# The fp32 products of a gated linear attention as f32r products of high and low parts

## What is computed

```python
proj = h @ w_in                                  # q, k, v, r, g_low
log_a = log_sigmoid(g_low @ w_gate_up + b_gate) / 16
cum = cumsum(log_a, axis=chunk);  total = cum[..., -1:, :]
k_dec = k * exp(total - cum);     chunk_decay = exp(total)
state = chunk_decay * state + k_dec^T v          # over the four chunks
o = q state                                      # then norm, silu(r), w_out
```

## Time and profile before

| | |
|---|---|
| median of 3 runs | 1426.6 us (1424.5 to 1426.8) |
| profiled execution, own time | 1427.55 us |
| its span (first to last instruction) | 1425.8 us |
| busy share of the span | PE 99%, DVE 60%, ACT 50%, POOL 2% |
| mean granted clock of TensorE | 0.997 of 2.4 GHz |
| read from HBM | 275.91 MB, 195 GB/s over the span |

### The profile page before, as it was taken

How to read it: one execution, slowest core, us unless ns; L and a number is a source line. 1 busy time by engine, 2 the same in 40 slices (tenths; PEclk the granted TensorE clock), 3 DMA queues, 4 the chain that set the end, 5 groups by cost and what they waited for, 6 DMA issues and landing times. The chain is left out here.

```text
span 1425.8 us, 17673 instructions
## 1 busy us (share of the span) xinstructions
PE 1418.1 (99%) x7202; PEld 1249.9 (88%) x7202; DVE 853.5 (60%) x889; ACT 717.9 (50%) x858; POOL 24.8 (2%) x44
## 2 busy tenths in 40 slices
PE   9999999999999999999999999999999999999999
PEld 7888888888899888998899888998888888888887
DVE  5555545655566655665555655565667786565654
ACT  6543544545545434544444534455564674665642
POOL 2000000000000000000000000000000001000000
PEclk9999999999999999999999999999999999999999
DMA  9555465657666666666666666666655556545574
GB/s 353 162 168 163 154 213 180 199 183 252 200 198 199 201 205 202 200 205 201 200 201 205 199 205 206 196 203 193 205 186 186 170 183 207 177 148 173 186 232 132
DMA packets 78016, 279.16 MB, mean 196 GB/s; under 512 B 8704, under 2 KB 9728, under 8 KB 77552
## 3 DMA queue, kind: packets, MB, share of 16 engines
q1 hardware_dynamic: 76000, 273.06, 59.4%
q0 software_dynamic: 784, 3.08, 0.6%
q10 hardware_dynamic: 1152, 1.90, 0.4%
HBM read 275.91 MB, written 2.10 MB: 195 GB/s over the span
## 5 line engine op out<-in xcount | busy, mean ns | idle before, releaser
L1020 DVE TENSOR_TENSOR w_lo<-raw,w_hi 128x1024 fp32r<-128x1024 f32 x508 | 620.0, 1224 | 521.4 <-ACT w_hi L722 517.5
L722 ACT ACTIVATE w_hi<-raw 128x1024 fp32r<-128x1024 f32 x508 | 535.0, 1056 | 642.2 <-PE banks L420 454.3
L418 PE MATMUL banks<-w_hi,xa 128*128 128x512 f32 x752 | 292.6, 389 | 0.5 <-DVE w_lo L1020 0.5
L418 PE MATMUL banks<-w_hi,xb 128*128 128x512 f32 x768 | 291.7, 380 | 0.0
L419 PE MATMUL banks<-w_lo,xb 128*128 128x512 f32 x768 | 291.1, 379 | 0.0
L420 PE MATMUL banks<-w_hi,xb 128*128 128x512 f32 x768 | 291.1, 379 | 0.0
L419 PE MATMUL banks<-w_lo,xa 128*128 128x512 f32 x752 | 285.8, 380 | 0.0
L420 PE MATMUL banks<-w_hi,xa 128*128 128x512 f32 x752 | 285.8, 380 | 0.0
L442 PE MATMUL banks<-xa,w_hi 128*128 128x512 f32 x1024 | 242.3, 379 | 0.0
L442 PEld LDWEIGHTS banks<-xa,w_hi 128*128 128x128 f32 x1024 | 184.3, 190 | 20.8
L420 PEld LDWEIGHTS banks<-w_hi,xb 128*128 128x128 f32 x768 | 145.2, 189 | 20.6
(11 more groups left out here) (196 smaller groups left out, 609.3 us busy)
## 6 DMA issues: line engine op xcount, KB each, us to landing
raw<-in_weights SPq DMA_DIRECT2D x511, 512.0 KB, 4.2
h<-in_x SPq DMA_DIRECT2D x2, 1024.0 KB, 10.1
arena<-in_x_turned SPq DMA_DIRECT2D x7, 256.0 KB, 6.3
result<-stage ACTq DMA_DIRECT2D x6, 256.0 KB, 4.7
arena<-in_final_norm POOLq DMA_DIRECT2D x1, 1024.0 KB, 7.2
raw<-in_weights SPq DMA_DIRECT2D x2, 256.0 KB, 5.0
arena<-in_gla_b_gate POOLq DMA_DIRECT2D x1, 512.0 KB, 8.5
arena<-in_lru_w_a POOLq DMA_DIRECT2D x1, 512.0 KB, 9.2
```

The source lines that it names most:

```text
L418: pe.matmul(o, xh[:, kt, xs], woven(w_hi, slot, k), start=kt == 0, stop=False)
L722: act.activation(w_hi[:, n % RING, :, :], raw[:, n % RING, :, :], ACT.Copy)\
L1020: dve.tensor_tensor(w_lo[:, n % RING, :, :], raw[:, n % RING, :, :], w_hi[:, n % RING, :, :].bitcast(F32), ALU.subtract).then_inc(lo_ready, 1)
```

## The change

All products of the four groups above become f32r products of high and low parts, and the parts have to be made:

- **Gate expansion.** ACT rounds `w_up_gate` twice, to rows 0 to 63 and 64 to 111 of `up_hi`, and DVE subtracts to `up_lo`, both at (0, 5). DVE splits `g_low` in two steps at (0, 6). Each of the four products becomes two f32r products. The load of `w_up_gate` has 64 rows instead of 48.
- **Span sums.** ACT rounds `log_a` to `la_hi` at (1, 5) and (1, 7), DVE subtracts to `la_lo` (`split_log`) at (1, 6) and (2, 0). 32 f32r products with 128 columns each (of which 7 are wanted) take the place of 16 fp32 products with 7, and move on PE from after (1, 7) to after (2, 0).
- **Suffix sums.** Eight f32r products after (2, 1), in four banks of PSUM, instead of two fp32 products after (2, 0) and two after (2, 2). ACT's exponentials move to c = 2 and 3, DVE's decayed keys to c = 3 and 4.
- **Sums over values.** ACT rounds the scores (four steps in place of two), DVE subtracts (four in place of two) one step later; ACT rounds both halves of the v panel, DVE subtracts for both. Nine f32r products for each head instead of three fp32 ones.
- GpSimd clears a larger `spans` and 32 rows of `g_low`, and casts `suffix`, at the start.

Operands that move through PE are stored or read so that neighbouring columns lie apart (`turns`, `pairs`), as those of the large products are (`woven`).

```diff
         ident = sb("ident", [P, P])
-        suffix = sb("suffix", [P, P])
+        suffix = sb("suffix", [P, P], F32R)
...
-        g_low = room(6144, S)
+        up_hi = nc.alloc_sbuf_tensor_at("up_hi", [P, 1024], F32R, offset=arena_at)
+        up_lo = nc.alloc_sbuf_tensor_at("up_lo", [P, 1024], F32R, offset=arena_at + 4 * 1024)
+        g_low = nc.alloc_sbuf_tensor_at("g_low", [P, S], F32R, offset=arena_at + 4 * 6144)
+        spans = nc.alloc_sbuf_tensor_at("spans", [P, TT, P], F32R, offset=arena_at + 4 * 14000)
+        la_hi = nc.alloc_sbuf_tensor_at("la_hi", [P, TT, 1024], F32R, offset=arena_at + 4 * 8704)
+        la_lo = nc.alloc_sbuf_tensor_at("la_lo", [P, TT, 1024], F32R, offset=arena_at + 4 * 10752)
...
-        scores = room(2816, GH, 384)
+        scores_hi = nc.alloc_sbuf_tensor_at("scores_hi", [P, GH, 384], F32R, offset=arena_at + 4 * 2816)
+        scores_lo = nc.alloc_sbuf_tensor_at("scores_lo", [P, GH, 384], F32R, offset=arena_at + 4 * 13760)
...
-        vals = room(6656, TT, N)
+        vals_hi = nc.alloc_sbuf_tensor_at("vals_hi", [P, TT, N], F32R, offset=arena_at + 4 * 6656)
+        vals_lo = nc.alloc_sbuf_tensor_at("vals_lo", [P, TT, N], F32R, offset=arena_at + 4 * 5376)
...
+        def turns(m):
+            return m.rearrange("p (a b) -> p b a", a=2)
+
+        def pairs(m):
+            return m.rearrange("p (b a) -> p b a", a=2)
+
+        SCORED = ((slice(0, 64), slice(0, S), slice(0, S)), (slice(0, 64), slice(S, S + P), slice(S + P, 2 * S)),
+                  (slice(64, 128), slice(64, S), slice(64, S)),
+                  (slice(64, 128), slice(S + 64, S + P), slice(2 * S - 64, 2 * S)))
...
             link(pool.memset(gate_w[:, :, :].bitcast(F32), 0.0))
-            pool.memset(spans[:, :, :], 0.0).then_inc(consts, 1)
-            triangle(suffix[:, :], 1.0 / 16, ALU.is_gt)
-            link(pool.affine_select(out=suffix[:, 0:CHUNK], in_=suffix[:, 0:CHUNK],
+            link(pool.memset(g_low[32:64, :].bitcast(F32), 0.0))
+            pool.memset(spans[:, :, :].bitcast(F32), 0.0).then_inc(consts, 1)
+            triangle(draft[:, 2, :], 1.0 / 16, ALU.is_gt)
+            link(pool.affine_select(out=draft[:, 2, 0:CHUNK], in_=draft[:, 2, 0:CHUNK],
                                     compare_op=ALU.is_ge, fill=0.0, base=CHUNK - 1,
...
+            pool.tensor_copy(suffix[:, :], draft[:, 2, :])
...
-            pool.dma_start(w_up_gate[0:LOW, :], w_gate_up).then_inc(up_in, 16)
+            pool.dma_start(w_up_gate[0:64, :], w_gate_up).then_inc(up_in, 16)
...
                 tt, half = divmod(i, 2)
                 if i == 0:
                     pe.wait_ge(low_out, 1)
-                    pe.wait_ge(up_in, 16)
-                pe.matmul(banks[:, gate_bank(i), :], g_low[0:LOW, tt * P:(tt + 1) * P],
-                          w_up_gate[0:LOW, half * N:(half + 1) * N], start=True, stop=True)\
-                    .then_inc(gate_ready, 1)
+                    pe.wait_ge(up_split, 1)
+                own, cols = slice(tt * P, (tt + 1) * P), slice(half * N, (half + 1) * N)
+                pe.matmul(banks[:, gate_bank(i), :], g_low[0:64 + LOW, own], turns(up_hi[0:64 + LOW, cols]),
+                          start=True, stop=False)
+                pe.matmul(banks[:, gate_bank(i), :], g_low[0:LOW, own], turns(up_lo[0:LOW, cols]),
+                          start=False, stop=True).then_inc(gate_ready, 1)

             def span_sums():
-                pe.wait_ge(log_ready, 2)
+                pe.wait_ge(gate_out, 4)
+                pe.wait_ge(la_split, 2)
                 for k in range(8):
-                    for tt in range(TT):
-                        last = pe.matmul(aux[:, 0, k * 7:(k + 1) * 7], log_a[:, tt, k * P:(k + 1) * P],
-                                         spans[:, tt, :], start=tt == 0, stop=tt == 1)
+                    for i, (part, tt) in enumerate(((la_hi, 0), (la_lo, 0), (la_hi, 1), (la_lo, 1))):
+                        last = pe.matmul(aux[:, k // 4, k % 4 * P:(k % 4 + 1) * P], part[:, tt, k * P:(k + 1) * P],
+                                         spans[:, tt, :], start=i == 0, stop=i == 3)
                 last.then_inc(span_ready, 1)

             def suffix_sums(i):
                 tt, half = divmod(i, 2)
-                if i == 0:
-                    pe.wait_ge(gate_out, 4)
-                if i == 1:
+                if i == 2:
                     pe.wait_ge(decay_ready, 1)
-                if i >= 2:
-                    pe.wait_ge(suf_out, i - 1)
-                pe.matmul(aux[:, (i + 1) % 2, :], suffix[:, :], log_a[:, tt, half * N:(half + 1) * N],
-                          start=True, stop=True).then_inc(suf_ready, 1)
+                for part in (la_hi, la_lo):
+                    last = pe.matmul(banks[:, 4 + i, :], suffix[:, :], turns(part[:, tt, half * N:(half + 1) * N]),
+                                     start=part is la_hi, stop=part is la_lo)
+                last.then_inc(suf_ready, 1)
...
-                pe.matmul(aux[:, 0, :], scores[:, hd, 0:P], vals[:, 0, :], start=True, stop=True)
-                pe.matmul(aux[:, 1, :], scores[:, hd, P:2 * P], vals[:, 0, :], start=True, stop=False)
-                pe.matmul(aux[:, 1, :], scores[:, hd, 2 * P:3 * P], vals[:, 1, :], start=False, stop=True)\
-                    .then_inc(o_ready, 1)
+                for i, tt, st in ((0, 0, 0), (1, 1, 0), (2, 1, 1)):
+                    own = slice(i * P, (i + 1) * P)
+                    for p, (s, v) in enumerate(((scores_hi, vals_hi), (scores_hi, vals_lo), (scores_lo, vals_hi))):
+                        last = pe.matmul(aux[:, tt, :], s[:, hd, own], turns(v[:, st, :]), start=p == 0 and st == 0,
+                                         stop=p == 2 and st == tt)
+                last.then_inc(o_ready, 1)
...
                     if c == 7:
                         for i in range(4):
                             gate_up(i)
-                if t == 1:
-                    if c == 7:
-                        span_sums()
                 if t == 2:
                     if c == 0:
-                        suffix_sums(0)
-                        suffix_sums(1)
-                    if c == 2:
-                        suffix_sums(2)
-                        suffix_sums(3)
+                        span_sums()
+                    if c == 1:
+                        for i in range(4):
+                            suffix_sums(i)
                     if c in (5, 7):
...
-                        act.activation(vals[:, 0, :], acc(q, 0), ACT.Copy, scale=rs[:, ST_X, 0:1])\
-                            .then_inc(acc_read_act, 1)
+                        for tt in range(TT):
+                            ins = act.activation(turns(vals_hi[:, tt, :]), pairs(acc(q, tt)), ACT.Copy,
+                                                 scale=rs[:, ST_X, tt:tt + 1])
+                        ins.then_inc(acc_read_act, 1)
                         act.wait_ge(acc_read_act, count("kqvruxKQVgl", q))
...
+                if t == 0 and c == 5:
+                    act.wait_ge(up_in, 16)
+                    act.wait_ge(tp_lo, CH)
+                    act.activation(up_hi[64:64 + LOW, :], w_up_gate[0:LOW, :], ACT.Copy)
+                    act.activation(up_hi[0:64, :], w_up_gate[0:64, :], ACT.Copy).then_inc(up_rounded, 1)
                 if t == 1:
+                    if c in (5, 7):
+                        act.wait_ge(log_ready, (c - 3) // 2)
+                        act.activation(la_hi[:, (c - 5) // 2, :], log_a[:, (c - 5) // 2, :], ACT.Copy)\
+                            .then_inc(la_rounded, 1)
...
-                    if c == 7:
+                if t == 2:
+                    if c == 1:
                         act.wait_ge(span_ready, 1)
-                        act.activation(decay.rearrange("p a b -> p (a b)"), aux[:, 0, 0:8 * 7], ACT.Exp)\
...
-                if t == 2:
-                    if c in (1, 3):
-                        for i in (c - 1, c):
+                    if c in (2, 3):
+                        for i in (2 * c - 4, 2 * c - 3):
                             tt, half = divmod(i, 2)
                             act.wait_ge(suf_ready, i + 1)
-                            act.activation(log_a[:, tt, half * N:(half + 1) * N], aux[:, (i + 1) % 2, :],
+                            act.activation(turns(log_a[:, tt, half * N:(half + 1) * N]), pairs(banks[:, 4 + i, :]),
                                            ACT.Exp).then_inc(suf_out, 1)
                     if c == 6:
                         move_first(key_t[:, 0:2, :], groups_before(2) + 1)
...
                     act.wait_ge(sc_ready, hd + 1)
-                    act.activation(scores[0:64, hd, 0:S], aux[0:64, hd % 2, 0:S], ACT.Copy)
-                    act.activation(scores[0:64, hd, S:S + P], aux[0:64, hd % 2, S + P:2 * S], ACT.Copy)\
-                        .then_inc(sc_act, 1)
+                    for rows, to, src in SCORED:
```

(52 more changed lines are left out.)

13 lines of the change are left out of this document (7 added, 6 removed).

## The result

| | before | after |
|---|---|---|
| median of 6 runs | 1426.31 us (1424.21 to 1427.51) | 1430.26 us (1429.22 to 1431.21) |
| ratio | | 1.0026, 95% interval 1.0016 to 1.0036 |
| profiled execution, own time | 1427.55 us | 1429.9 us |
| its span | 1425.8 us | 1428.1 us |
| mean granted clock | 0.997 | 0.995 |

The change makes the kernel slower by 3.95 us by the medians, 0.26% by the ratio, which is outside the range that was given (1419.0 to 1428.9).

A forecast was written before the change was run, and what follows sets the result against it. TensorE's work was taken to bound the kernel: 14.4 us before against 15.3 after, +0.9, with -2.5 for the values gave -1.6 us, 1425.9 against the profiled execution and 1425.0 against the median; range 1419.0 to 1428.9.

The forecast's parts named there:

- What bounds the kernel: Whole kernel: the sum of TensorE's work; ACT and DVE work counts only where TensorE waits for it.
- where the wait comes: Ahead of the span sums: TensorE, free at 57.15 us, waits 6.7 us for both halves of `la_lo`.
- The queues as laid out: ACT's and DVE's steps up to the second half of `la_lo`, listed with times; span sums start at 63.8 us.
- Gate expansion: Gate products, from 32.11 us: eight f32r products take 1.75 us instead of 3.7, a gain of 2.0 us.
- The clock: Span sums after the wait: half clock for 1.3 to 4.0 us costs 0.7 to 2.0 us, taken as 1.6.
- rival 2: Span sums and main products behind: the clock stays down, slower than before; net +2.3, 1428.9 us; chance 0.17.
- prices of the span sums: Span sums before the change: 5.0 us, plus 2.2 behind them at half clock, the clock back at 65.64.
- The sum: Whole kernel: -1.6 us against the profiled 1427.55, less 0.95 for its distance above the median, gives 1425.0 us.
- Suffix sums: Suffix sums: four fp32 products, 3.4 us, become eight f32r, 1.75, a gain of 1.7 us.
- sums over values: Each head: nine f32r products take 1.94 us instead of 2.57; -2.5 us for four heads.
- the work on ACT and DVE elsewhere: Added steps for gates, keys, scores and v panels: covered, priced at zero; exponentials stay 0.6 us each.

The follow-up runs named there:

- e9_gates: The changed kernel with its eight gate products run over all 128 rows, the added rows being zeros: 1430.64 us, ratio 1.0027.
- e8_fill: The changed kernel with 22 unread products of 512 columns on TensorE ahead of the span sums: 1425.68 us, ratio 0.9999.
- e3_rows: e2_cover with the eight gate products run over all 128 rows, the added rows being zeros: 1422.75 us, ratio 0.997.
- e2_cover: The changed kernel with DVE's second log-gate low part made earlier and the span sums one chunk later, after (2, 1): 1419.11 us, ratio 0.9947.
- e5_order: e3_rows with DVE doing the second tokens' log gate, then both log-gate low parts, then low part (1, 6): 1418.86 us, ratio 0.9946.
- e10_turn: The changed kernel with only DVE's order of e5_order, span sums staying after (2, 0): 1422.52 us, ratio 0.9971.
- e6_narrow: e2_cover with 8 columns instead of 128 in each product of the span sums: 1422.72 us, ratio 0.9973.

## Why the prediction was wrong

**What bounds the kernel, and where the wait comes.** Right. TensorE's work is the time, and the one new wait is at the span sums, for the second half of `la_lo`. The queues as laid out gave 63.8 us for the start of the span sums; it was 63.91. Each step of DVE came within 0.2 us of the list (low part (1, 5) 54.9, measured 55.05; first low part of the log gates 56.05, 56.19; last one 62.5, 62.54). The three reads that carried this, one step's distance in each queue and which step stands behind which, were in the earlier trace rows. That the start came out to 0.1 us is in part luck. In e9_gates and e8_fill, with the same queues, DVE began that low part at 63.07 and 63.35 where it was 62.54, and the delay is there from the split for which ACT waited for weights from HBM: it began at 31.27 and 31.54 where it was 30.72. In the sum the wait was 1.6 us too long (5.1, not 6.7), because TensorE came that much later from the gates.

**Gate expansion: mis-sized.** "Eight f32r products are 1.75 us" took the pace of products with 128 rows for products with 112 and 48. They took 3.3; the four fp32 products before, of 48 rows, took longer than four times 0.86 as well, and I passed over that in the earlier trace rows: 3.7 us is 0.27 more. e3_rows shows that the rows are the cause. It moved the total by nothing, since the wait shrank by the same 1.6 us; e9_gates shows that directly.

**The clock: the step that failed.** "Half clock for 1.3 to 4.0 us ... I take 1.6" assumed that the span products, of the shape of transposes, bring the clock back while they run. They did not in 6.86 us; it came back only after 4.9 us of main products. The term of 1.6 us for the clock measured 5.8, 3.4 in the span sums and 2.5 behind them, and it alone is 4.2 of the 5.3 us between 1425.0 and 1430.26. That is rival 2, whose mechanism came in full: 6.9 us at 0.214 a product, where it said 7.0, and a further 2.5 behind, where it said 2.0. I had given it 0.17 because the transposes at the start reached full pace. In the profile after, these same 26 transposes took 5.81 us instead of 4.47 for the whole of them, 0.22 apart to the end:

```profile
1.59 5.81 PE L713 MATMUL banks<-ident 128*128 128x128 f32 x26 [1.59 <-POOL ident L351]
```

In the thirteen profiles they took 4.38 to 5.81 us. So the row I leaned on was one execution's outcome. (That they ran at half clock is inferred from their pace; the profile's clock column reads 1.00 in both traces there.) I also misread: a mean of 0.55 over 65.6 to 66.0 puts the return of the clock near 65.96, not at 65.64 as stated with the prices of the span sums, so it came 4.4 us after dense products began, not 4.0, which makes the 2.0 of rival 2 the 2.2 that the chunk behind had shown. A mechanism on which two rows disagree, the 7-column products of the earlier trace rows and those transposes, deserved more than one chance in six.

**The Trainium skill** asks (TensorE: Matmul & The Clock Gate, Why this matters for your kernels) for no gaps between bursts of products, as they bring the half clock back. The trace agrees: a rest of 5.1 us, and half clock behind it. Its other figure, about 81 ns for sustained pairs of weight load and 128-column product (Back-to-back issue gap), is not borne out: 112 ns at full clock in e2_cover.

**The sum.** Rival 2 gave +2.3 us against the profiled execution, and the two profiled executions differ by 1429.9 - 1427.55 = 2.35. It became 1428.9 because I took off 0.95, the distance of that execution of before from its median. That was wrong for a kernel whose clock falls each time. The changed kernel has no such distance: its profiled execution lies 0.36 below its median. 0.95, 0.36 and 0.05 are the 1.4 us up to 1430.26. The faster runs of before are those in which its clock held, by the mean clocks of the 67 executions above; all six of the changed kernel are at 0.995 or 0.996.

**Suffix sums, sums over values, the work on ACT and DVE elsewhere:** as forecast: 1.7 us, 1.95 for a head, and no wait. One price was wrong without effect: ACT's and DVE's steps that read PSUM in order and write neighbouring columns 256 columns apart take 1.12 to 1.17 us for 512 columns, not 0.6 to 0.7. The row that I used for the exponentials was of another pattern. The room there was larger than the error.

## What to carry to other kernels

On a kernel that is the sum of TensorE's work, ask of each new wait not how long it is but what stands behind it: here 4.2 us less rest were worth 11 us, because the products behind the rest ran at half clock and did not bring it back. What is won ahead of such a wait is lost in it, so the first thing to lay out is the queue of the engine that ends the wait; another order of VectorE's steps was worth 7.7 us here, more than all the cheaper products together (1.7 + 2.5 at the suffix sums and the values, and what the gates gave).

## What the runs showed of the hardware that was not expected

- **f32r products of 112 and 48 rows in turn did not overlap their weight loads.** They came 0.41 us from one to the next; the same eight products over 128 rows with zeros: 0.216 (e3_rows, e9_gates). Whether it is the fewer rows or the change from 112 to 48 that does it was not tried.
- **32 products of 128 columns, each with its own weight load, neither raised the clock nor, alone, lowered it.** At 1.00 before them, 3.6 us of them left it at 1.00 in e2_cover, e5_order and e10_turn with waits of 0.4 to 0.9 us ahead of them; with 1.2 it fell in e3_rows, with 0.9 in e8_fill. At 0.50 before them, 6.86 us of them left it there. Between executions of one such kernel the time differs by 3 to 4 us (e3_rows, e8_fill), and the mean clock of each differs with it. What decides it in one execution was not found.
- **Eight columns cost what 128 do** where each product has its own weight load, 0.11 us (e6_narrow), and keep the clock less often: it stayed up in one of eight executions, in five of five with 128 (e2_cover).
- **The clock can fall without a rest.** In the profiled execution of e10_turn it was down from 36.3 to 39.8 us, behind eight gate products of 112 and 48 rows, with TensorE at work throughout; the cause was not tried.
- **Writing neighbouring columns 256 columns (1 KB) apart** costs ACT and DVE 1.12 to 1.17 us for 512 columns: the exponentials took 1.12 (mean of four) and, on columns in order in the kernel before, 0.59; the two parts of the values 1.16 on ACT and 1.17 on DVE, which also reads the high part so, and in order before 0.67 and 0.75. The strided read of 1024 columns in the earlier trace rows, 1.01, is not of that kind.
